# Block attention: queries, second keys and first probabilities turned by a block exchange through device memory and full-width VectorE turns

## The reference, cut to what matters

```python
q, k, v = jnp.split(h @ w_in, 3, axis=-1)
...
q = partial_rope(q, pos) * (Dh ** -0.5)
k = partial_rope(k, pos)
...
s_own = jnp.einsum('bhnid,bhnjd->bhnij', qb, kb).astype(jnp.float32)
s_own = jnp.where(causal, s_own, NEG)
m_own = jnp.max(s_own, axis=-1)
p_own = jnp.exp(s_own - m_own[..., None])
l_own = jnp.sum(p_own, axis=-1)
o_own = jnp.einsum('bhnij,bhnjd->bhnid', p_own, vb)
...
m_sel, l_sel, o_sel = lax.map(attend_selected, (q_ch, sel_ch, val_ch))
...
o = (o_own * a[..., None] + o_sel * b[..., None]) / (l_own * a + l_sel * b)[..., None]
return o.astype(h.dtype) @ w_out
```

## Time and profile before

| | |
|---|---|
| runs | 1100.97, 1100.97, 1100.49 us; median 1100.97 |
| the profiled execution, its time | 1100.77 us |
| its span in the trace | 1098.8 us |
| mean granted clock of PE | 0.999 |
| PE busy | 1090.5 us (99%) |
| DVE busy | 843.9 us (77%) |
| ACT busy | 663.9 us (60%) |
| POOL busy | 194.9 us (18%) |
| moved by DMA | 214.6 MB, 195 GB/s over the span |
| chain that ended last | PE 93%, DVE 4%, ACT 1%, issue 1% |

### The profile page before, as it was taken

One profiled execution on the slowest core, in us unless ns is written; L12 is line 12 of the kernel. 1 busy time (PEld: TensorE's weight loads), 2 busy tenths in 40 slices (PEclk: granted clock), 3 DMA queues, 4 the chain that ended last, 5 costly groups with the idle time before them and its releaser, 6 DMA issues.

```text
span 1098.8 us, 12971 instructions
## 1 busy us (share of the span) xinstructions
PE 1090.5 (99%) x5095; PEld 906.3 (82%) x5095; DVE 843.9 (77%) x956; ACT 663.9 (60%) x811; POOL 194.9 (18%) x135
## 2 busy tenths in 40 slices
PE   9999999999999999999999999999999999999997
PEld 7788888888888888888888888888888888888886
DVE  5785668776569998678538569999677976799974
ACT  6646566654767765654588366576455645655651
POOL 1434700000343420000013000004306000000430
PEclk9999999999999999999999999999999999999999
DMA  9745444545555489655534546459855344544970
GB/s 350 250 171 191 132 172 154 215 173 191 177 194 206 168 207 317 228 215 190 193 115 170 194 173 245 175 171 259 296 191 215 106 163 171 203 180 160 251 240 38
DMA packets 31800, 214.60 MB, mean 195 GB/s; under 512 B 3768, under 2 KB 3936, under 8 KB 6912
## 3 DMA queue, kind: packets, MB, share of 16 engines
q1 hardware_dynamic: 28320, 195.61, 48.9%
q0 software_dynamic: 3424, 18.23, 8.0%
HBM read 212.77 MB, written 1.05 MB: 195 GB/s over the span
## 4 chain that ended last, share of the span: by engine, by line
PE 93%; DVE 4%; ACT 1%; issue 1%; DMA 0%; SPq 0%; DVEq 0%; ACTq 0%
PE ps L789 77%; PE ps L1318 3%; PE aux L862 3%; PE ps L1266 2%; PE aux L1266 2%; PE ps L1320 1%; DVE Wl L2044 1%; PE ps L905 1%; PE aux L1111 1%; PE aux L1355 1%; PE aux L1096 1%; ACT Wh L1484 1%; PE ps L982 0%; PE aux L1342 0%; DMA mrows<-in_mem 0%
## 5 line engine op out<-in xcount | busy, mean ns | idle before, releaser
L789 PE MATMUL ps<-Wh,xT 128*128 128x512 f32 x1792 | 559.9, 391 | 0.0
L2044 DVE TENSOR_TENSOR Wl<-raw,Wh 128x2048 fp32r<-128x2048 f32 (+1 forms) x188 | 437.4, 2336 | 126.6 <-ACT Wh L1484 125.0
L1484 ACT ACTIVATE Wh<-raw 128x2048 fp32r<-128x2048 f32 (+1 forms) x192 | 366.0, 1914 | 169.7 <-PE ps L789 155.8
L789 PEld LDWEIGHTS ps<-Wh,xT 128*128 128x128 f32 x1792 | 336.4, 188 | 69.8 <-issue 0.3
L789 PE MATMUL ps<-Wl,xT 128*128 128x512 f32 x896 | 348.6, 389 | 0.0
L789 PEld LDWEIGHTS ps<-Wl,xT 128*128 128x128 f32 x896 | 168.3, 188 | 34.1
L2652 DVE STREAM_TRANSPOSE htmp<-held 32x512 f32<-32x512 f32 x128 | 89.9, 703 | 2.5
L789 PE MATMUL ps<-Wh,hTh 128*128 128x512 f32 x192 | 74.8, 390 | 0.0
L789 PE MATMUL ps<-Wh,hTl 128*128 128x512 f32 x192 | 74.7, 389 | 0.0
L789 PE MATMUL ps<-Wl,hTh 128*128 128x512 f32 x192 | 74.7, 389 | 0.0
L693 POOL DMA_DIRECT2D raw<-in_wstream x12 | 10.7, 890 | 249.6 <-DVE Wl L2044 249.6
(11 more groups left out here) (419 smaller groups left out, 1537.8 us busy)
## 6 DMA issues: line engine op xcount, KB each, us to landing
raw<-in_wstream SPq DMA_DIRECT2D x182, 1024.0 KB, 4.8
raw<-in_wstream POOLq DMA_DIRECT2D x12, 1024.0 KB, 8.6
grow<-in_post_gains POOLq DMA_DIRECT2D x4, 512.0 KB, 5.9
grow<-in_b_gate POOLq DMA_DIRECT2D x6, 256.0 KB, 3.5
mrows<-in_mem SPq DMA_DIRECT2D x2, 512.0 KB, 5.5
raw<-in_wstream SPq DMA_DIRECT2D x2, 512.0 KB, 6.7
x<-in_x SPq DMA_DIRECT2D x1, 1024.0 KB, 14.7
out<-x SPq DMA_DIRECT2D x4, 256.0 KB, 2.0
```

The costliest lines, as they stand in the source:

```text
L789: mm = nc.tensor.matmul(ps[2 * pair + t][:, :], a[:, kt, t * P:(t + 1) * P], w[:, slot, j, :], start=(first and j == 0 and q == 0), stop=( ...
L1484: nc.scalar.activation(split_view(Wh, g), weight_view(raw, g), ACT.Copy).then_inc(hi_ready, 1)
L2044: nc.vector.tensor_tensor(split_view(Wl, g), weight_view(raw, g), split_view(Wh, g).bitcast(F32), ALU.subtract).then_inc(lo_ready, 1)
```

## The change

The second keys, both halves of the queries and the probabilities of heads 0 to 3 are no longer turned piece by piece or by PE. A turn of a 128x128 matrix is split in two steps: an exchange of 32x32 blocks between groups of 32 partitions, and a turn inside each block.

- Queries and second keys: ACT writes the rows in an order of 32-column chunks (`cut_rows`; the keys' scale is folded in there by the new scalar `x4_keys`). SP stores them to a line in device memory, one DMA for each group of 32 partitions (`cut_out`, four DMAs of 128 KB), and loads them back with the chunk on the partition (`cut_in`, one DMA of 512 KB). DVE then turns all blocks in one instruction over 128 partitions (`turn_moved`) straight into bqT or bkT. SP issues these DMAs between five weight loads, ahead of the loads of positions moba2 + 7 to moba2 + 11.
- Probabilities of heads 0 to 3: DVE turns the blocks first, in one instruction (`turn_first_probs`, 2048 elements a partition), ACT's own DMA queue stores them (four DMAs of 256 KB) and loads them back (one of 1 MB, `turned_p`); PE reads its moving operand from there in runs of 32 columns (`moba_first_out`).
- PE loses 8 turns of the second keys and 16 of the probabilities, ACT the copies of both, DVE two copies and 32 turns of queries. The first keys and the probabilities of heads 4 to 7 are turned as before.
- New waits: PE's second scores wait for the count 4 of `bqk_turned` (first queries, probabilities, second queries, second keys, in that order on DVE), its first value products for `p_in`; ACT waits for the landing of the four stores ahead of its load back, which stands in front of the split of mobao1's first granule.

```diff
+            def cut_out(name, rows, ready, count):
+
+                sp.wait_ge(sem(ready), count)
+                for q in range(4):
+                    sp.dma_start(bline[name][:, :, q, :].rearrange("c i e -> i c e"),
+                                 rows[32 * q:32 * q + 32, :, :, :, :].rearrange("p c h t j -> p c (h t j)"))\
+                        .then_inc(sem("line_out"), 16)
+
+            def cut_in(name):
+
+                n = LINES + list(bline).index(name)
+                sp.wait_ge(sem("line_out"), 64 * n + 64)
+                if n:
+                    sp.wait_ge(sem("line_in"), 16 * n)
+                sp.dma_start(bmoved[name][:, :, :, :].rearrange("p q b j -> p q (b j)"),
+                             bline[name].rearrange("c i q e -> (c i) q e")).then_inc(sem("line_in"), 16)
+
             for g in range(RING, NP):
+                if g == P0["moba2"] + 7:
+                    cut_out("q0", BQ[:, 0, :, :, :, :], "bq_rot", 1)
+                elif g == P0["moba2"] + 8:
+                    cut_in("q0")
...
+                elif g == P0["moba2"] + 11:
+                    cut_out("k1", BK1[:, :, :, :, :], "bk_rot", 2)
+                    cut_in("k1")
...
             product("moba4", (xTh, xTl))
-            turn_keys(1)
-            for h in range(4):
-                turn_probs("bpT", h, bprob, "b_prob")
-
             def second_scores():
-                pe.wait_ge(sem("bq_turned"), 2)
-                wait_operand("bkT1", range(2))
+                pe.wait_ge(sem("bqk_turned"), 4)
...
             wait_drained(pe, "moba4", 1)
+            pe.wait_ge(sem("p_in"), 16)
             for h in range(4):
-                moba_out(h)
+                moba_first_out(h)
...
-            def second_turned():
-                bk_turned(1)
+            def first_probs():
+                act.wait_ge(sem("bqk_turned"), 2)
+                for q in range(4):
+                    act.dma_start(bline["p"][:, :, q, :].rearrange("c i e -> i c e"),
+                                  blocks_p[32 * q:32 * q + 32, :, :, :].rearrange("p c b j -> p c (b j)")).then_inc(sem("p_line"), 16)
                 rows("moba4", lambda t: BV[:, 0, t, :], "x4")()
 
-            unit("moba4", second_turned)
+            unit("moba4", first_probs)
+            act.wait_ge(sem("p_line"), 64)
+            act.wait_ge(sem("bqk_turned"), 3)
+            act.dma_start(turned_p[:, :, :, :, :, :].rearrange("p q h t k j -> p q (h t k j)"),
+                          bline["p"].rearrange("c i q e -> (c i) q e")).then_inc(sem("p_in"), 16)
...
-            turn_queries(0, 0, 8)
-            unit("moba2", lambda: turn_queries(0, 8, 16))
-            turn_queries(1, 0, 8)
+            def turn_moved(name, dst):
+
+                dve.wait_ge(sem("line_in"), 16 * (LINES + list(bline).index(name)) + 16)
+                nc.vector.transpose(dst.rearrange("p h (t q j) -> p (h t) q j", q=4, j=32),
+                                    bmoved[name][:, :, :, :].rearrange("p q b j -> p b q j")).then_inc(sem("bqk_turned"), 1)
+
+            unit("moba2")
+            turn_moved("q0", bqT[:, 0:4, :])
...
+            unit("moba3", None, *(lambda h=h: masked_max(h) for h in range(4)), *(lambda h=h: moba_probs(h) for h in range(4)),
+                 turn_first_probs, lambda: turn_moved("q1", bqT[:, 4:8, :]))
+            turn_moved("k1", bkT[:, 4:8, :])
+            unit("moba4")
```

More of the change, by code:

```diff
@@ L1406, in _ @@
             product("moba2", (xTh, xTl))
[L1408 to L1413, removed]
+            pe.wait_ge(sem("bk_rot"), 1)
+            for b in range(2):
+                turn_rows("bkT0", BK0, b)
             product("moba3", (xTh, xTl))
-            pe.wait_ge(sem("bq_turned"), 1)
+            pe.wait_ge(sem("bqk_turned"), 1)
             wait_operand("bkT0", range(2))
@@ L1431, in _, with moba_values, moba_first_out @@
             product("moba5", (xTh, xTl), before={1: second_scores})
+            def moba_values(h, ks):
+                return BV[:, h // 4, ks, (h % 4) * HD:(h % 4 + 1) * HD]
+            def moba_first_out(h):
+                o = open_aux("boT", h)
+                for ks in range(2):
+                    for t0, t1 in ((0, 1), (1, 2)) if h == 3 and ks else ((0, 2),):
+                        mm = nc.tensor.matmul(o[:, t0 * P:t1 * P], moba_values(h, ks),
+                                              turned_p[:, :, h, t0:t1, ks, :].rearrange("p q t j -> p t q j"),
+                                              start=(ks == 0), stop=(ks == 1), skip_group_check=True)
+                done(mm, "boT", h)
             def moba_out(h):
                 wait_read(pe, "bpT", h)
-                attend("boT", h, lambda ks: BV[:, h // 4, ks, (h % 4) * HD:(h % 4 + 1) * HD], bpT)
+                attend("boT", h, lambda ks: moba_values(h, ks), bpT)
             wait_drained(pe, "moba4", 1)
+            pe.wait_ge(sem("p_in"), 16)
             for h in range(4):
-                moba_out(h)
+                moba_first_out(h)
             def second_heads():
@@ L1968, in _, with cut_rows, go @@
             square_sums("x4", x, junk[:, :])
[L1969 to L1980, removed]
+            def cut_rows(name, dst, scale):
+                def go():
+                    if scale == "x4_keys":
+                        act.wait_ge(sem("rs_scaled"), 2)
+                    else:
+                        act.wait_ge(sem("norm_rstd"), NORMS["x4"])
+                    for t in range(2):
+                        wait_unit(act, name, t)
+                        nc.scalar.activation(dst[:, :, :, t, :].rearrange("p c h j -> p h c j"),
+                                             bank(name, t).rearrange("p (h c j) -> p h c j", c=4, j=32), ACT.Copy,
+                                             scale=S(scale, t, t + 1)).then_inc(drained["act"], 1)
+                return go
+            unit("moba0", cut_rows("moba0", BQ[:, 0, :, :, :, :], "x4_rstd"))
+            unit("moba1", rows("moba1", lambda t: BK0[:, t, :], "x4"))
+            unit("moba2", cut_rows("moba2", BQ[:, 1, :, :, :, :], "x4_rstd"))
+            for b in range(2):
+                o = wait_aux(act, "bkT0", b)
+                free(nc.scalar.activation(bkT[:, 2 * b:2 * b + 2, :], o[:, :], ACT.Copy, scale=float(HD) ** -0.5), "bkT0", b)
+            unit("moba3", cut_rows("moba3", BK1[:, :, :, :, :], "x4_keys"))
             def moba_exps(h):
@@ L2730, in _, with turn_first_probs @@
             unit("moba0")
+            dve.wait_ge(sem("norm_rstd"), NORMS["x4"])
+            nc.vector.tensor_scalar(S("x4_keys"), S("x4_rstd"), HD ** -0.5, None, ALU.mult).then_inc(sem("rs_scaled"), 1)
             unit("moba1")
[L2733 to L2742, removed]
[L2744 to L2746 removed]
+            def turn_moved(name, dst):
[4 more added lines that the diff above has]
+            turn_moved("q0", bqT[:, 0:4, :])
+            def turn_first_probs():
+                dve.wait_ge(sem("b_prob"), 8)
+                dve.wait_ge(sem("line_out"), 64 * LINES + 128)
+                nc.vector.transpose(blocks_p[:, :, :, :].rearrange("p c b j -> p b c j"),
+                                    bprob[:, :, :, :].rearrange("p h t (k c j) -> p (h t k) c j", c=4, j=32))\
+                    .then_inc(sem("bqk_turned"), 1)
             def masked_max(h):
```

39 lines of the change are left out of this document (21 added, 18 removed).

## The result

The changed kernel takes **1104.91 us** (median of 6 runs, 1104.49 to 1105.87); the kernel before, on the same chip, 1100.76 (1100.49 to 1100.97). The ratio is 1.0039 with an interval of 1.0029 to 1.0049: slower by some 4.2 us, where 1100.2 was forecast and 1102.5 was the range's upper end. The profiled execution is the slowest of the six, 1105.87, with a span of 1103.9, so the profile shows a loss of 5.1 us against the profiled execution before.

A forecast was written before the change was run, and what follows sets the result against it. DVE's chain was taken to bound the change: heads 4 to 7 start 0.78 us earlier, not 2.54, so 1100.77 becomes 1099.99; with the median 0.20 above the profiled execution, 1100.2. Range 1098.4 to 1102.5.

The forecast's parts named there:

- the one on ACT: ACT ahead of mobao1's Wh: stores land after 4.8 us at 879.1, Wh done 881.66 against 881.95 wanted; just free.
- The load back: Probabilities' load on ACT's queue: lands at 883.9 to 887.7; PE wants it at 886.09, can bear 888.2; free.
- rival 2: ACT held at the probabilities' landing, or load back beyond 888.2: at 8.6 us, +2.8 in all, 1103.7; chance 0.13.
- Rival 4: PE's clock falls in the 2.15 us idle time before mobao0: costs 2.1, sum +1.3, 1102.3; chance 0.07.
- DVE's turns: Three wide turns in DVE's chain, by a fit of earlier rows: probabilities 2.30, others 1.24 each, 4.78 us together.
- The start of heads 0 to 3: DVE's maxima start when head 0's scores are there: 859.76 in place of 862.45.
- The chain to mobao1's split: DVE's turns and splits in order reach the split of mobao1's first granule at 881.95, heads 4 to 7 at 884.16.
- The second scores: PE's second scores wait for the fourth turn, 877.53 against their start at 877.99: free.
- SP's part: SP's stores and loads back between weight loads, 12.0 us each: 851.1, 862.9, 874.6; all free, keys' margin 1.7 us.
- the 32-column runs: PE's value products of heads 0 to 3 read their moving operand in 32-column runs: no change taken from 3.63 us.
- the sum itself: Whole kernel: -0.78 us from the profiled 1100.77 gives 1099.99; 1100.2 as the median.
- Rival 1: PE's saving stays whole, -2.54: 1098.4; needs DVE 1.76 us shorter, for example by cheaper turns; chance 0.10.

The follow-up runs named there:

- experiment 1: Changed kernel with SP issuing no weight load from moba2 + 11 on until the probabilities are loaded back: 1099.96 us, ratio 0.9991 to the kernel before.
- experiment 2: Changed kernel with 23 matmuls keeping PE busy ahead of its wait for the probabilities: 1103.28 us, ratio 1.0022 to the kernel before.
- experiment 5: Changed kernel with SP's weight loads held only from moba2 + 12 on, so one runs beside the round trip: 1101.24 us, ratio 1.0003 to the kernel before.
- 7: Kernel of experiment 4 with DVE's maxima of heads 4 to 7 moved ahead of two weight splits: 1100.48 us, ratio 0.9996 to the kernel before.
- 6: Kernel of experiment 1 with DVE's maxima of heads 4 to 7 moved ahead of two weight splits: 1099.91 us, ratio 0.9991 to the kernel before.
- experiment 9: Kernel of 6 with DVE's last split moved behind the copies bpT of heads 5 and 7: 1098.49 us, ratio 0.9978 to the kernel before.
- experiment 4: Changed kernel with probabilities sent SBUF to SBUF in 16 SP transfers ahead of the weight loads, no device memory: 1099.71 us, ratio 0.9992 to the kernel before.

## Why the prediction was wrong

**The step that failed** is the one on ACT: "after 4.8 (all four are 1 MB together) 879.1", and behind it "The load back lands 4.8 to 8.6 later, 883.9 to 887.7 ... Free". The last store took 6.58 us instead of 4.8, and landed at 881.15 instead of 879.1; the load back took 10.0, above both ends of its bounds, and landed at 891.18, 3.0 us past the 888.2 that PE could bear. Of these two the load back decides: from the measured landing of the stores, 881.15, and with the 4.7 of experiment 1, it would have been there at 885.9, before PE wants it at 886.09.

The price came from the earlier trace rows, which are medians over all weight loads of the kernel, whatever moves beside them. For a transfer that has the engines to itself it was right, 4.8 and 4.7 in experiment 1; what failed is to take it for a transfer that shares them. The upper end, 8.6, was another queue's, and no bound for a transfer that shares. What was missing is the stretch itself: SP's timeline and the DMA share of 876 to 888 in the kernel before, with four loads of 1 MB in it. The prediction had the sentence ("weight loads run at the same time"), put it as a point for rival 2, and priced with it only ACT's hold at a late store, not the load back.

**What came is two rivals together.** Rival 2 closed with "A late load back, beyond 888.2, ends the same way"; that is the first 2.8 us: mobao0 at 894.67 in experiment 2, against 891.87 worked out. Its other half, ACT held at the landing, is there too: a landing after 879.4 was to pass to DVE, 1.75 us by the measured landing, and heads 4 to 7 start 1.62 later than worked out. It costs nothing further only because the load back is later still. That rival 2's time, 1103.7, lies near the measured one is luck: it was worked out from that hold, with the 8.6 of POOL's queue. Rival 4, the clock, adds 2.97 in the profiled execution (1.6 between the medians). It was priced at 2.1 for a wait of 2.15 us, which was the wrong wait: 1.88 us in experiment 5 and 1.96 in 7 left the clock at 1.00, and the 5.2 us lowered it. The chances of 0.13 and 0.07 were given as if the two excluded each other; a late transfer makes the wait that brings the clock down. The Trainium skill (TensorE: Matmul & The Clock Gate, "What's actually happening") has the direction right, an idle TensorE is put back to 1.2 GHz, and the rows agree with 0.50.

**What was right.** DVE's turns: 2.31, 1.20 and 1.24 against 2.30 and 1.24 taken, so the fit from the earlier trace rows holds over 128 partitions. The Trainium skill (VectorE: DVE Perf Modes, "The three transpose paths") gave 311 ns for 128x128, an estimate of 9.95 us for the three; the rows show 4.75. The page's figure is not at odds with them, its use as a rate was: by the fit of the earlier trace rows, as an estimate, one instruction on 128 elements a partition costs 0.30 us (the rows are f32, the page's figure bf16), of which 0.17 is paid once an instruction, and the 9.95 pays it 32 times. The start of heads 0 to 3: 859.7 (859.68 against 859.76). The chain to mobao1's split: 881.9 in both. The second scores, SP's part and the 32-column runs: free, as said. POOL's rotation of the second queries ended 2 us later (852.82); SP's stores waited for it, and neither DVE's turn of them at 872.98 nor PE did.

**And the sum itself.** With the loads held (experiment 1) the change has all its parts and none of the sharing, and takes 1099.96, 0.91 less than before; -0.78 was worked out. The waits are not quite as drawn (0.21, 0.52 and 0.94, in place of one of 2.15), but DVE's chain is what bounds it, as experiments 6 and 9 show by moving it. Rival 1, PE's saving whole, was nearly reached (2.3 of 2.54, experiment 9) not by a cheaper turn but by held loads and another order of the splits. The working was a good account of PE, ACT and DVE, and left out what the DMA engines were already moving.

What stays open: why the changed kernel's median runs lie 1.0 to 1.2 us under its two profiled ones. A clock that came back earlier, or a load back that landed earlier, would do it; only the profiled executions show either. The clock fell in all eleven runs of it: their mean granted clock is 0.995 to 0.997, that of every run of the other kernels in the experiments 0.998 to 1.000.

## What to carry to other kernels

Price a new transfer on the critical path by what moves in that very stretch, not by the median landing of its kind: list the loads of all queues there, and if the DMA share is near 1.0, hold back those with slack until the urgent one has landed (one wait on SP was worth 5 us here; letting one of four loads through gave 1.2 of it away). When a late input makes TensorE wait as long as here (5.2 us; 1.96 left the clock alone), add the clock to the price of the wait. And when an engine that is 99% busy is relieved, follow the next engine's order to the end, since each wait that is removed uncovers the next (experiments 6 and 9).

## What the runs showed of the hardware

- A 1 MB load on ACT's queue landed after 10.0 us beside a stream of 1 MB loads on SP's queue, 7.1 with one of them let through, and 4.7 with none; from 882 to 892 its packets took 24.8% of the engines' time, those of SP's queue 73.9%.
- The granted clock stayed at 1.00 through waits of 1.88 and 1.96 us, fell to 0.50 late in a wait of 5.21, and was 0.50 in two more windows with PE at work throughout (2.00 of 2.00 us); 18 matmuls took 6.61 us instead of 3.63.
- Four DMA issues on ACT's queue took 2.75 us, 0.69 each on average (0.35 the first, 1.26 the last), where 0.47 was taken.
- A transfer of 64 KB from SBUF to SBUF landed after 2.0 us (median; 2.9 at most in experiment 4), and 16 of them took SP 10.76 us to issue, 0.67 each. From the first issue at 874.16 to PE's start at 886.41 it was 12.25 us, so most of this exchange's time is issuing.
